# Differential attention: two other banks for the first head-norm sums, and four instructions moved in three engine queues

## The reference, cut to what matters

```python
q = rms_norm((xn @ w_q).reshape(B, S, DIFF_HEADS, 2, DIFF_DH), q_gain) * (DIFF_DH ** -0.5)
k = rms_norm(k.reshape(B, S, DIFF_HEADS, 2, DIFF_DH), k_norm)
s = einsum('bhcqd,bhckd->bhcqk', q_blk, k)          # causal mask, then softmax over keys
a = p[:, :, 0] - lam * p[:, :, 1]
o = einsum('bhqk,bhkv->bhqv', a, v)
o = rms_norm(o, head_gain) * (1.0 - lambda_init)
return o.reshape(B, S, DIFF_HEADS * DIFF_VD) @ w_out
```

## Time and profile before

| | before |
|---|---|
| median of 3 runs | 2290.1 us (2289.8 to 2290.17) |
| profiled execution, its own time | 2290.38 us |
| span of that execution | 2288.6 us |
| granted TensorE clock over the span | 1.0 of full speed |
| PE busy | 2274.8 us, 99% |
| DVE busy | 1129.6 us, 49% |
| ACT busy | 896.5 us, 39% |
| DMA | 206.55 MB, mean 90 GB/s |

### The profile page before, as it was taken

How to read it: one execution, slowest core, us unless ns; L and a number is a source line. 1 busy time by engine, 2 the same in 40 slices (tenths; PEclk the granted TensorE clock), 3 DMA queues, 4 the chain that set the end, 5 groups by cost and what they waited for, 6 DMA issues and landing times.

```text
span 2288.6 us, 26310 instructions
## 1 busy us (share of the span) xinstructions
PE 2274.8 (99%) x10810; PEld 1851.7 (81%) x10810; DVE 1129.6 (49%) x1739; ACT 896.5 (39%) x1420; POOL 0.2 (0%) x4
## 2 busy tenths in 40 slices
PE   9999999999999999999999999999999999999999
PEld 7777888888778888888888888888887767888887
DVE  5655543444575443445677654334344786432432
ACT  5654322223464322223534543223234885331321
POOL 0000000000000000000000000000000000000000
PEclk9999999999999999999999999999999999999999
DMA  3222222322222222322311132322232112232222
GB/s 140 85 84 74 92 87 89 111 93 88 92 88 87 98 81 98 108 86 92 117 61 65 56 111 92 104 99 92 92 106 85 56 56 74 92 101 102 92 92 92
DMA packets 36695, 206.55 MB, mean 90 GB/s; under 512 B 4192, under 2 KB 5216, under 8 KB 17248
## 3 DMA queue, kind: packets, MB, share of 16 engines
q1 hardware_dynamic: 34128, 199.43, 25.8%
q10 hardware_dynamic: 2448, 5.44, 0.7%
HBM read 202.76 MB, written 2.10 MB: 90 GB/s over the span
## 4 chain that ended last, share of the span: by engine, by line
PE 96%; DVE 2%; ACT 1%; issue 1%; DMA 0%; SPq 0%; ACTq 0%; DVEq 0%
PE ps L320 29%; PE ps L322 29%; PE ps L321 29%; PE ps L1076 2%; PE ps L1712 1%; PE ps L2132 1%; PE ps L1131 1%; PE ps L2151 1%; PE ps L1100 1%; PE ps L1126 1%; PE ps L1092 0%; DVE low_w L346 0%; PE ps L2142 0%; PE ps L584 0%; ACT swa_p L1223 0%
## 5 line engine op out<-in xcount | busy, mean ns | idle before, releaser
L320 PE MATMUL ps<-xh,high_w 128*128 128x512 f32 x1592 | 632.1, 397 | 0.8 <-DVE xl L489 0.6
L322 PE MATMUL ps<-xh,low_w 128*128 128x512 f32 x1592 | 620.9, 390 | 0.0
L321 PE MATMUL ps<-xl,high_w 128*128 128x512 f32 x1592 | 620.4, 390 | 0.0
L346 DVE TENSOR_TENSOR low_w<-raw_w,high_w 128x2048 fp32r<-128x2048 f32 (+3 forms) x208 | 423.0, 2035 | 170.0 <-ACT high_w L338 169.6
L338 ACT ACTIVATE high_w<-raw_w 128x2048 fp32r<-128x2048 f32 (+3 forms) x208 | 353.3, 1700 | 289.0 <-PE ps L322 281.5
L320 PEld LDWEIGHTS ps<-xh,high_w 128*128 128x128 f32 x1592 | 299.2, 188 | 66.4 <-issue 6.1
L322 PEld LDWEIGHTS ps<-xh,low_w 128*128 128x128 f32 x1592 | 299.0, 188 | 63.1
L321 PEld LDWEIGHTS ps<-xl,high_w 128*128 128x128 f32 x1592 | 299.4, 188 | 60.7 <-issue 1.4
L321 PE MATMUL ps<-ffn_hidl,high_w 128*128 128x512 f32 x864 | 336.4, 389 | 0.0
L322 PE MATMUL ps<-ffn_hidh,low_w 128*128 128x512 f32 x864 | 336.4, 389 | 0.0
L320 PE MATMUL ps<-ffn_hidh,high_w 128*128 128x512 f32 x864 | 336.4, 389 | 0.0
(11 more groups left out here) (289 smaller groups left out, 2448.1 us busy)
## 6 DMA issues: line engine op xcount, KB each, us to landing
raw_w<-in_w_f_gu SPq DMA_DIRECT2D x44, 1024.0 KB, 4.9
raw_w<-in_w_m_up SPq DMA_DIRECT2D x32, 1024.0 KB, 4.9
raw_w<-in_w_m_dn SPq DMA_DIRECT2D x32, 1024.0 KB, 4.9
raw_w<-in_w_f_dn SPq DMA_DIRECT2D x32, 704.0 KB, 4.1
raw_w<-in_w_b_qk SPq DMA_DIRECT2D x8, 1024.0 KB, 4.8
raw_w<-in_w_e_qk SPq DMA_DIRECT2D x4, 1024.0 KB, 5.1
raw_w<-in_w_e_out SPq DMA_DIRECT2D x4, 1024.0 KB, 5.3
raw_w<-in_w_o_q SPq DMA_DIRECT2D x8, 512.0 KB, 3.6
```

The costliest lines, as they stand in the source:

```text
L320: pe.matmul(out, sh, mh, start=start, stop=False)
L321: pe.matmul(out, sh, ml, start=False, stop=False)
L322: return pe.matmul(out, sl, mh, start=False, stop=stop)
L346: dve.tensor_tensor(wl[slot][:, 0:elems], raw[slot][:, 0:elems], wh[slot][:, 0:elems].bitcast(F32), ALU.subtract).then_inc(w_split, 1)
```

## The change

1. `sums` of head 0 write banks 2 and 3 in place of 0 and 1 (`sum_bank`), and `root` reads them there. Banks 0 and 1 then come free with `raw`, so `made` of head 1 waits for `raw_staged` in place of `logged`.
2. `sums(0, 1)` leaves `project` and stands in step 0 behind the first two k tiles of `made(1, 0)`, as in the other steps.
3. In step 0 DVE's `raw(1, 1)` stands ahead of `combine` of rows (0, 1). In the other steps it stays behind.
4. `head_sum(p-2)` stands behind `scores` of rows (2, 3), in steps 2 to 7.
5. In the last step ACT's `place_values` stands at the beginning of the step.
6. In step 6 DVE's `split(0)` stands ahead of the last `combine`.

```diff
         def step(p, st, nx, prev):        # PE
-            if p == 0:
-                made(nx[0], 0, 0, 6)
-            elif nx:
+            if nx:
                 head = 1 if key_split(p) else 2
                 made(nx[0], 0, 0, head)
                 sums(p, 1)
...
+            scores(p, st, (2, 3))
             if past_two(p):
                 head_sum(p - 2)
-            scores(p, st, (2, 3))
...
         def project(p, st):
             sums(p, 0)
-            sums(p, 1)
...
+    def sum_bank(p, which):
+        return which if p else 2 + which
...
-            if first == 0:
+            if first == 0 and p == 1:
+                pe.wait_ge(F["raw_staged"], 1 + which)
+            elif first == 0:
                 wait_past(pe, F["logged"], 2 * p - 1 + which)
...
         def step(p, st, nx, prev):        # ACT
             if nx:
                 round_weights(act, st_diff.base + p + 2)
+            else:
+                place_values(prev[0])
             exps(p, st, (0, 1))
...
                 copy_pt(prev[0], (2, 3))
+            if prev and nx:
                 place_values(prev[0])
...
             norm(p, st)                   # DVE
+            if p == 0:
+                raw(nx[0], 1)
             combine(p, st, (0, 1))
+            if prev and nx:
+                raw(nx[0], 1)
             if nx:
-                raw(nx[0], 1)
                 normed(nx[0], nx[1], 0)
             combine(p, st, (2,))
             if nx:
                 square_low(nx[0], 1)
+            if p == NHD - 2:
+                split(0)
             combine(p, st, (3,))
...
             if p == NHD - 2:
-                split(0, 1, 2)
+                split(1, 2)
```

More of the change, by code:

```diff
@@ L2107, in sums @@
         def sums(p, which):
+            bank = sum_bank(p, which)
             pe.wait_ge(F["blocks_rounded"], 1)
@@ L2112, in sums @@
                 pe.wait_ge(F["squared"], 2 * p + 2)
-                last = pe.matmul(ps[:, 1, :], blockones[:, :], sq[:, 1, :], start=True, stop=True)
+                last = pe.matmul(ps[:, bank, :], blockones[:, :], sq[:, 1, :], start=True, stop=True)
             else:
                 pe.wait_ge(F["k_low" if which else "q_low"], p - 1 if which else p + 1)
-                pe.matmul(ps[:, which, :], blockones_r[:, :], f_high[:, :], start=True, stop=False)
-                last = pe.matmul(ps[:, which, :], blockones_r[:, :], sqr[:, which, :], start=False, stop=True)
+                pe.matmul(ps[:, bank, :], blockones_r[:, :], f_high[:, :], start=True, stop=False)
+                last = pe.matmul(ps[:, bank, :], blockones_r[:, :], sqr[:, which, :], start=False, stop=True)
             last.then_inc(F["sums_made"], 1)
@@ L2252, in root @@
                 wait_past(act, H["scaled"], p - 2)
-            act.activation(sq[:, 2 + which, :], ps[:, which, :], ACT.Ln, bias=eps[:, 0:1],
+            act.activation(sq[:, 2 + which, :], ps[:, sum_bank(p, which), :], ACT.Ln, bias=eps[:, 0:1],
                            scale=1.0 / 64).then_inc(F["logged"], 1)
```

## The result

The changed kernel takes 2293.47 us (median of 21 runs, 2292.57 to 2293.92), the kernel before 2289.87 us in the same sessions (21 runs, 2289.24 to 2290.49): 3.6 us more, ratio 1.0015 with a 95% interval of 1.0009 to 1.0021. The forecast was 0.6 us less, with a range up to 2290.9; the time lies above it, on the other side. It is within 0.2% of before, which had 0.97. The interval is 0.06% to either side of the ratio, so the 3.6 us (0.16%) are clear of the noise, although the prediction took some 0.2% for the least that can be told.

A forecast was written before the change was run, and what follows sets the result against it. PE's work bounds the kernel, so edits win only its waits, some 4 us. Gains 1.14 + 0.3 + 0.45 + 0.1 = 2.0, less 1.4 lost: 0.6 less, median 2289.5 us; range 2287.6 to 2290.9.

The forecast's parts named there:

- The step that failed: Middle steps, ACT: the later head sum delays `head_root` by 0.44 us, covered by 1.12 idle before the keys' square; cost nil.
- the third: Sign that the prediction is wrong: middle steps longer than before, where 19.0 us was forecast for 19.1.
- Head sum behind the scores: Steps 2 to 6, PE: head sum fills the wait before the transposes; gain 0.09 us a step, 0.45 in five.
- The last step: Last step: late head sum delays ACT's exponentials and DVE's chain, with no cover; PE loses 1.4 us, bounds 0 and 1.9.
- Lead: Before the first scores: sums in other banks and keys' sum behind two tiles fill PE's wait; gain 1.14 us.
- Raw keys first: Step 0, DVE: `raw` ahead of the first `combine` brings the keys' sum sooner; gain 0.3 us, bounds 0 and 0.54.
- Split: Before the output projection: first `split` 0.6 us sooner, most of PE's 0.27 wait met again; gain 0.1 us.
- Values first: Last step, ACT: values copied at the start remove a wait before the products, but a later wait absorbs it; gain nil.
- The one that ended on the slower side: Rival: ACT's 0.44 us slip reaches PE in each middle step through the keys' square; 2291.7 us, chance 0.08.

The follow-up runs named there:

- e3_own_buffers: Changed kernel with three buffers of their own for the head's square, high and low part, and no query-square wait for the head sum; 2288.98 us.
- e1_sum_back: Changed kernel with the head sum ahead of the scores of rows (2, 3) again, all else as changed; 2288.18 us.
- e5_lead_only: Kernel before with only the lead's sums in banks 2 and 3 and the keys' sum behind two tiles; 2288.62 us.
- e9: Changed kernel with head sum ahead of scores, one k tile ahead of the transposes, keys' sum behind two tiles in every step, no added buffers; 2286.04 us.
- e7: Kernel of e6 with the keys' sum behind two k tiles in place of one in steps 2 to 6; 2285.65 us.
- e2_sum_alone: Kernel before with only the head sum moved behind the scores of rows (2, 3); 2295.03 us.
- e6: Kernel of e3_own_buffers with the head sum ahead of the scores in the last step only; 2287.61 us.

## Why the prediction was wrong

**The step that failed** is the one that priced ACT's share of the moved head sum in the middle steps: "In the middle steps ACT reaches `head_root` late anyway [...] and ACT slips by 0.44", "Cost nil". It took `head_root` for the only instruction on ACT that waits for the head sum. `square(nx, 0)`, two instructions earlier in the queue, waits for it too (`wait_past(act, H["summed"], p - 2)`), since the square and the rounding right behind it use the head's buffers again: the rounding overwrites `diff_high`, which the head sum still has to read. Before, the head sum ended 0.3 us ahead of the square (1809.44 + 0.40 against 1810.13), and so the trace of before shows no such wait; I listed who waits for the moved instruction by the trace, not by the code. The slip was 1.73 us, not 0.44 (6.20 less 4.47). It moved two consumers. The copies for the next transposes came too late by 0.74, which I had not priced. The idle time before the keys' square fell from 1.12 to 0.35 and did not run out, but the keys' sum came 0.09 later behind its tile than in e3_own_buffers (1840.16 to 1840.73 against 1838.52 to 1839.00). Together that is the 0.83 between the steps of the two kernels. So the five steps cost 3.3 in place of gaining 0.45. e3_own_buffers takes this wait away, with the buffers that made it needed, and leaves every queue's order; it lands 1.05 under before, where the forecast said 0.6. Of the prediction's own signs of being wrong, it was the third that showed: longer middle steps.

The Trainium skill, "Perfetto Trace Analysis", section "Optimization Strategy", says that the same gap repeating on the engine that should be saturated can mean that on-chip memory for the next tile is short, by buffer count. Here it does: the repeated 0.74 us gap of PE went with three more 512-column buffers, though the engine that waited for the buffer was ACT and PE only stood behind it.

**Head sum behind the scores, in itself** gained 0.13 a step, forecast 0.09. From the last k tile to the row behind the transposes' first follower, e3 takes 3.16 (1826.23 to 1829.39) where before took 3.29, and e1_sum_back, which lacks only edit 4, has steps of 19.03 to 19.09 for e3's 18.94. The transposes start 0.23 behind a rounded matmul, as the forecast's 0.24 had it.

**The last step** went as forecast and a little dearer: 1.47 for 1.4. ACT and DVE there, against the earlier trace rows:

```profile
1887.66 0.08 DVE L2418 DVE_READ_ACCUMULATOR2_ANT small<- 128x1 f32 x1
...
1892.89 0.20 DVE L2426 RECIPROCAL small<-small 128x8 f32<-128x8 f32 x1 [2.29 <-ACT diff_p L2267]
```

```profile
1888.47 0.69 ACT L2300 ACTIVATE squares_sq<-ps,eps 128x512 f32<-128x512 f32 x1 [1.99 <-PE ps L316]
1889.19 0.63 ACT L2303 ACTIVATE squares_sq<-squares_sq 128x512 f32<-128x512 f32 x1
1889.72 0.60 ACT L2267 ACTIVATE diff_p<-diff_p,small 128x384 f32<-128x384 f32 x1
```

ACT is idle 1.99 us (forecast about 2) while the mask for the exponentials behind it is ready at 1887.74, and takes them at 1889.72, in program order. The Trainium skill's rule that the prediction cites ("TensorE: Matmul & The Clock Gate", section "Architectural detail: the array is 16× 32×32, not 1× 128×128"), a strict first-in first-out queue on ScalarE, agrees with this row. Both losses came by that order: in each, ready work stood behind one instruction that waited.

**Lead:** 1.25 for 1.14; 0.07 of the difference lies ahead of the keys' sum, which starts 1.62 behind the query sum (1745.94 to 1747.56) where 1.69 was forecast. **Raw keys first:** 0.3 for 0.3. **Split:** 0.13 for 0.1. **Values first:** nil for nil. With the head sum's own 0.13 in five steps and the 1.47, these terms give 0.85 of the 1.05 that e3 measured. The rest is about the 0.04 a step by which steps 2 to 5 of e1_sum_back and e5_lead_only are under before as well; no run places it.

**The rivals.** The one that ended on the slower side was nearest: a slip of ACT that reaches PE in each middle step. It had 0.08, was tied to the wrong consumer (the keys' square; it was the copies of the transposed blocks) and to a slip of 0.44, so its 2291.7 was still short. The range left it out, and the time fell outside.

## What to carry to other kernels

When an instruction is moved later, look in the code for every wait on its semaphore, the ones that guard a buffer it reads included: a wait that was always met leaves no trace in the profile of before, and it is the one that binds after. On an engine with one queue its cost is not the wait but everything that stands behind it, so the slack to compare it with is that of the nearest consumer further down. To fill a wait of the engine that bounds, take work for which nobody waits soon: a tile of the next projection filled here the same wait as the head sum, and the steps came out as short (18.62 in e9 and in e7).

## What the runs showed of the hardware

- Profiled executions reach the attention at times up to 0.75 us apart (the lead's query sum at 1745.94 in the changed kernel and 1746.69 in e2_sum_alone, one execution of each), with the same instructions ahead of it. A single span therefore can't settle a difference of half a microsecond; step lengths inside the profile can.
- On PE, a full-fp32 score matmul starts 0.32 us behind a rounded one (1809.44 to 1809.76 before), and a transpose 0.23 behind one (1832.15 to 1832.38 in e3), which is also what separates two rounded ones. A pause ahead of a rounded matmul costs more than itself: behind it the next one starts 0.31 later, not 0.23 (1838.83 to 1839.14 in e6, 1837.82 to 1838.04 in e7).
